# A two-block sequence model on one core: the products with 64 rows and 128 columns of weights in the two chunked recurrences, each made as two products of 64x64

## The chip, the cores and the metric

The kernel runs on one core of one Trainium2 chip, in float32 throughout. The metric is the device time of one execution in microseconds (us), the median of several. Below, PE is TensorE's matmul queue, PEld its weight loads, DVE is VectorE, ACT ScalarE, POOL GpSimd, SP the engine that issues the DMAs.

## The reference

Two blocks stand one behind the other, on 1024 tokens of width 1024. The first has two layers; each layer projects the normed input and runs three branches: a gated delta rule (GDN, 6 heads of 64), a latent attention (MLA) and an RWKV-7 recurrence (4 heads of 64). The second block is one with a gated convolution and a gated linear recurrence. The change touches the GDN and RWKV recurrences alone. The core of the GDN one, in chunks of c tokens, for both directions at once:

```
def step(s, inp):
    w_c, u0_c, p_c, qg_c, kd_c, ge_c = inp
    u = u0_c - jnp.einsum('nhcd,nhde->nhce', w_c, s)
    o = jnp.einsum('nhcd,nhde->nhce', qg_c, s) + jnp.einsum('nhij,nhje->nhie', p_c, u)
    s = ge_c[..., None, None] * s + jnp.einsum('nhcd,nhce->nhde', kd_c, u)
    return s, o
```

and the RWKV one, written token by token in the reference and made in chunks by the kernel:

```
sa = jnp.einsum('nhij,nhj->nhi', s, -kk_t)
s = s * w_t[:, :, None, :] + sa[..., None] * b_t[:, :, None, :] + v_t[..., None] * k_t[:, :, None, :]
y = jnp.einsum('nhij,nhj->nhi', s, r_t)
```

## The kernel before

The kernel works in stages with a barrier between them; in each layer of the first block the opening projections are followed by the stage `rw_chunk` (lines 722 to 1411, at 176 to 425 us of the span in layer 0), the GDN front, and the stage `gdn_chunk` (lines 1613 to 2237, at 573 to 890 us). Every engine runs its own written-out list of functions, and they meet by semaphore counts; the order of TensorE's list is the order of its work.

Both chunk stages cut the 1024 tokens into 8 chunks of 128 and take 8 steps s = 0 to 7; the forward direction takes chunk s and the backward one chunk 7 - s in the same step. A unit is a direction e and a pair of heads m: the two heads h = 0 and 1 of a pair lie in partitions 0 to 63 (LOW) and 64 to 127 (HIGH). RWKV has 4 units (8 products of one kind a step), GDN has 6 (12 products). A step consists of:

- `keys_on_state`: keys (weights, 64 rows of head width, 128 columns of tokens) times the state (64x64), added in the banks RB and RB + 1 to what `values_in` put there. In GDN `values_in` is the turning of the values, against a negative identity, of the same shape; in RWKV it is a product with 128 rows.
- `right_side` on ScalarE and VectorE copies the result out (R), `first_half` multiplies one half of the chunk by its inverse (64x64 products), the result is copied (W), `across` takes it to the other half (64x64), that is copied (R2), `second_half` multiplies again (64x64), and that is copied (W).
- `to_state` (128 rows, 64 columns) makes the new state, which VectorE copies or adds (Zc in RWKV, S in GDN); the next step's `keys_on_state` waits for it.
- `out_known` (RWKV) and `out_of_state` (GDN): queries (64 rows, 128 columns) times the old state, into the pair of banks of the step's output; `out_of_chunk` adds the part of the chunk itself (128x128 weights).

Steps 0 to 3 also hold the preparation of steps 4 to 7: `pairs` and `keys`, whose results VectorE masks and ScalarE takes apart (`take_out`, the rows of G, AT5, AT6). After steps 0 to 3 come `fill`, projections that cover VectorE's inverses of the next four chunks, and `join`, 32x32 products on four row groups in turn. Steps 4 to 7 have nothing of this kind in them. Pairs of banks are used in turn, by the list TURNS; `claim` waits until the last user's result has been copied out.

In the two heads h the output goes to bank b + h, so the two row halves write different banks.

Of the kernel before, what the change touches and what calls it, by code (L numbers as in the profile page):

```python
# [33 lines left out]
GH, GD = 6, 64  # L34
# [5 lines left out]
RH, RD = 4, 64  # L40
# [96 lines left out]
def build(nc, io, values):  # L137
    with ExitStack() as ctx:
# [23 lines left out]
        def sbuf(stack, name, shape, dt=F32):  # L162
            n = named.get(name, 0)
            named[name] = n + 1
            return stack.enter_context(nc.sbuf_tensor(f"{name}_again{n}" if n else name, shape, dt))
# [30 lines left out]
        ps = ctx.enter_context(nc.psum_tensor("ps", [P, 8, 512], F32))  # L196

        def cst(name, k=None):
            a, n = C_AT[name]
            return consts[:, a:a + n] if k is None else consts[:, a + k * P:a + (k + 1) * P]  # L200
# [21 lines left out]
        for L in range(DEPTH):  # L222
# [5 lines left out]
            with ExitStack() as st:  # L228
# [493 lines left out]
                with ExitStack() as st2:  # L722
# [4 lines left out]
                    KR = sbuf(st2, "KR_w", [P, 5, 4, 2, P])  # L727
# [29 lines left out]
                    Zc = sbuf(st2, "Zc_w", [P, 2, 4, RD])  # L757
                    rwm = sbuf(st2, "rwm", [P, 8 * P])
                    RB, WB, SB = 4, 6, 7
                    MID = P // 2  # L760
                    RATE = float(np.exp(-0.5))
                    LOW, HIGH = slice(0, 64), slice(64, 128)

                    def masked(s):
                        if s % 5 in (1, 2):
                            return mt_own[:, s % 5 - 1]
                        n = {0: 0, 3: 1, 4: 2}[s % 5] * 3072
                        return hflat[:, n:n + 3072].rearrange("p (u k n) -> p u k n", u=8, k=3)

                    def chunk(s, e):  # L770
                        return NT - 1 - s if e else s

                    def tok(s, e):
                        return slice(chunk(s, e) * P, chunk(s, e) * P + P)
# [29 lines left out]
                    def v_of(s, e, u):  # L804
                        return vt_all[:, chunk(s, e), RD * u:RD * u + RD]
# [16 lines left out]
                    with nc.Block() as block:  # L822
                        @block.tensor
                        def _(pe):
                            def claim(name):
                                old = used_before(name)
                                if old is not None and old[0] == "p" and old[1] != "c":
                                    pe.wait_ge(*VEC["MT" + old[1:]])
                                elif old is not None and old[0:2] == "kt":
                                    pe.wait_ge(*ACT[old])  # L830
                                elif old is not None and old[0:4] in ("fill", "late"):
                                    pe.wait_ge(*ACT[old])
                                elif old is not None and old[0:2] == "pc":
                                    pe.wait_ge(*(VEC if old[-1] == "1" else ACT)[old])
                                elif old is not None:
                                    pe.wait_ge(*ACT[old])
                                    pe.wait_ge(*VEC[old])
                                return pair_of_banks(name)
# [59 lines left out]
                            def keys_on_state(s):  # L898
                                pe.wait_ge(*VEC[f"Zc{s}"])
                                for em in range(4):  # L900
                                    for h in range(2):
                                        c0 = slice(64 * h, 64 * h + 64)
                                        q = pe.matmul(ps[:, RB + h, RD * em:RD * em + RD], lhsT=KR[c0, s % 5, em, 0, :], rhs=Zc[c0, s % 2, em, :], start=False,
                                                      stop=False, skip_group_check=True)
                                q.then_inc(*PE(f"R{s}"))

                            def first_half(s):
# [55 lines left out]
                            def out_known(s):  # L963
                                b = claim(f"o{s}")
                                for em in range(4):
                                    for h in range(2):
                                        c0 = slice(64 * h, 64 * h + 64)
                                        pe.matmul(ps[:, b + h, RD * em:RD * em + RD], lhsT=KR[c0, s % 5, em, 1, :], rhs=Zc[c0, s % 2, em, :], start=(em == 0),
                                                  stop=False, skip_group_check=True)
                                for em in range(4):  # L970
                                    for h in range(2):
                                        pe.matmul(ps[:, b + h, RD * em:RD * em + RD], lhsT=masked(s)[:, 2 * em + h, 2, :], rhs=v_of(s, em // 2, 2 * (em % 2) + h),
                                                  start=False, stop=False, skip_group_check=True)
# [38 lines left out]
                            for s in range(4):  # L1012
                                keys_on_state(s)
                                to_state_known(s)
                                pairs(s + 4, 0)
                                first_half(s)
                                pairs(s + 4, 1)
                                across(s)
                                pairs(s + 4, 2)
                                second_half(s)  # L1020
                                if s < 3:
                                    values_in(s + 1)
                                out_known(s)
                                to_state(s)
                                out_of_chunk(s)
                                pairs(s + 4, 3)
                                keys(s + 4)
# [389 lines left out]
            with ExitStack() as st:  # L1417
                gq = sbuf(st, "gq", [P, 9, SEQ])
# [8 lines left out]
                S = sbuf(st, "S_g", [P, 2, 6, GD])  # L1427
# [185 lines left out]
                with ExitStack() as st2:  # L1613
# [11 lines left out]
                    KQ = wflat.rearrange("p (a b m n) -> p a b m n", a=2, b=2, m=6)  # L1625
# [6 lines left out]
                    RB, WB, SB = 4, 6, 7  # L1632
# [22 lines left out]
                    LOW, HIGH = slice(0, 64), slice(64, 128)  # L1655
# [18 lines left out]
                    with nc.Block() as block:  # L1674
                        @block.tensor
                        def _(pe):
# [69 lines left out]
                            def values_in(s):  # L1746
                                for em in range(6):
                                    e, m = em // 3, em % 3
                                    for h in range(2):
                                        c0 = slice(64 * h, 64 * h + 64)  # L1750
                                        pe.matmul(ps[:, RB + h, GD * em:GD * em + GD], lhsT=gq[c0, 6 + m, tok(s, e)], rhs=cst("nident")[c0, c0], start=(em == 0),
                                                  stop=False, skip_group_check=True)

                            def keys_on_state(s):
                                pe.wait_ge(*VEC[f"KQ{s}"])
                                if s:
                                    pe.wait_ge(*VEC[f"S{s - 1}"])
                                for em in range(6):
                                    e, m = em // 3, em % 3
                                    for h in range(2):  # L1760
                                        c0 = slice(64 * h, 64 * h + 64)
                                        q = pe.matmul(ps[:, RB + h, GD * em:GD * em + GD], lhsT=KQ[c0, s % 2, e, 3 + m, :], rhs=S[c0, s % 2, em, :], start=False,
                                                      stop=False, skip_group_check=True)
                                q.then_inc(*PE(f"R{s}"))

                            def first_half(s):
# [48 lines left out]
                            def out_of_state(s):  # L1815
                                b = claim(f"o{s}")
                                for em in range(6):
                                    e, m = em // 3, em % 3
                                    for h in range(2):
                                        c0 = slice(64 * h, 64 * h + 64)  # L1820
                                        pe.matmul(ps[:, b + h, GD * em:GD * em + GD], lhsT=KQ[c0, s % 2, e, m, :], rhs=S[c0, s % 2, em, :], start=(em == 0),
                                                  stop=False, skip_group_check=True)

                            def out_of_chunk(s):
                                b = pair_of_banks(f"o{s}")
# [31 lines left out]
                            for s in range(4):  # L1857
# [4 lines left out]
                                if s < 3:  # L1862
                                    diff(s + 1, 1)
                            decays(0)
                            values_in(0)
                            for n in range(NT - 1):
                                fill(n)
# [2213 lines left out]
```

## Time and profile before

| | |
|---|---|
| time, median of 3 runs | 3975.13 us (3971.03 to 3977.76) |
| the profiled execution: its own time | 3983.26 us |
| its span | 3981.3 us |
| TensorE busy | 3652.6 us (92%), 24920 matmul records |
| TensorE weight loads | 2272.2 us (57%) |
| VectorE / ScalarE / GpSimd busy | 2247.3 (56%) / 1249.7 (31%) / 283.1 us (7%) |
| mean granted TensorE clock | 0.954 |

### The profile page before, as it was taken

The page shows a single profiled execution, that of the slowest core. Times are in us where ns is not written, and L with a number is a line of the kernel's source. Part 1 is how long each engine was busy: PE and PEld are TensorE (multiplying, and loading weights), DVE is VectorE, ACT ScalarE, POOL GpSimd, SP SyncE. Part 2 cuts the span into 40 slices and gives each one's busy share as a digit, 9 for nine tenths or more (in the row PEclk, how much of TensorE's full clock was granted, in tenths as well). Part 3 has the DMA queues.
Part 4 walks back from the last instruction along what each step waited for, and adds up shares of the span by engine and source line. Part 5 has one row for each costly group of instructions (what it writes and reads, how often), then busy time and mean ns, then how long its engine had stood idle before and what let it go on. Part 6 is the DMA issues. An engine that isn't in the chain of part 4 may idle for free. (4 is left out here: it accounts for less than half of the span.)

```text
span 3981.3 us, 60111 instructions
## 1 busy us (share of the span) xinstructions
PE 3652.6 (92%) x24920; PEld 2272.2 (57%) x24920; DVE 2247.3 (56%) x3955; ACT 1249.7 (31%) x2191; POOL 283.1 (7%) x233
## 2 busy tenths in 40 slices
PE   7889988988989979897997998899999997999999
PEld 4467535775654457744766664466666665444443
DVE  3475467835663456456764565356666667533453
ACT  3253354314531234245433453212222222231001
POOL 0010000000000011010000000022222222000000
PEclk9899999979999989998988999999999999999999
DMA  4223212102032333311212004211111110322331
GB/s 154 97 86 104 76 37 79 59 24 90 13 110 98 118 92 92 121 32 41 70 57 108 9 11 147 80 35 43 43 43 43 43 33 22 121 61 75 98 106 52
DMA packets 301822, 281.14 MB, mean 71 GB/s; under 512 B 18016, under 2 KB 274144, under 8 KB 301552
## 3 DMA queue, kind: packets, MB, share of 16 engines
q1 hardware_dynamic: 301552, 277.30, 21.6%
q8 instruction: 199, 3.26, 0.3%
q14 instruction: 71, 0.58, 0.0%
HBM read 203.93 MB, written 73.33 MB: 70 GB/s over the span
## 5 line engine op out<-in xcount | busy, mean ns | idle before, releaser
L3386 DVE SCALAR_TENSOR_TENSOR cv<-glu,params,cv 128x1024 f32<-128x1024 f32 x240 | 361.0, 1504 | 6.4
L1471 PE MATMUL ps<-hT,w_cols 128*128 128x512 f32 x576 | 254.9, 602 | 13.6 <-PEq L158 13.6
L399 PE MATMUL ps<-hT,w_cols 128*128 128x512 f32 x448 | 204.5, 617 | 3.3 <-PEq L158 3.3
L1471 PEld LDWEIGHTS ps<-hT,w_cols 128*128 128x128 f32 x576 | 110.9, 193 | 152.7 <-issue 150.8
L3682 PE MATMUL ps<-hT,wr 128*128 128x512 f32 x360 | 161.7, 592 | 0.0
L399 PEld LDWEIGHTS ps<-hT,w_cols 128*128 128x128 f32 x448 | 88.3, 199 | 116.4 <-issue 116.4
L3362 POOL TENSOR_TENSOR Sp<-Sp,Rp 128x520 f32<-128x520 f32 (+1 forms) x56 | 88.5, 1580 | 565.4 <-DVE W L3403 565.4
L3145 PE MATMUL ps<-hT,w_f 128*128 128x347 f32 x384 | 117.2, 465 | 6.8 <-DMA w_f<-in_w_in 6.8
L3160 PE MATMUL ps<-w_i,hT 128*128 128x128 f32 x1024 | 120.7, 277 | 0.0
L3682 PEld LDWEIGHTS ps<-hT,wr 128*128 128x128 f32 x360 | 68.4, 190 | 86.1 <-issue 86.1
L3160 PEld LDWEIGHTS ps<-w_i,hT 128*128 128x128 f32 x1024 | 116.1, 192 | 2.2 <-issue 1.6
L3145 PE MATMUL ps<-hT,w_glu_a 128*128 128x347 f32 x384 | 114.2, 456 | 0.4 <-ACT sgb L3326 0.4
L3152 PE MATMUL ps<-hT,w_g 128*128 128x512 f32 x256 | 114.1, 599 | 0.0
L2999 PE MATMUL ps<-w_out,mT 128*128 128x512 f32 x256 | 114.0, 604 | 0.0
L3145 PE MATMUL ps<-hT,w_glu_b 128*128 128x347 f32 x384 | 113.4, 454 | 0.0
L2999 PE MATMUL ps<-w_out_again,mT_again 128*128 128x512 f32 x256 | 113.2, 601 | 0.0
L3152 PE MATMUL ps<-hT,w_q 128*128 128x512 f32 x256 | 111.2, 592 | 0.0
L3682 PE MATMUL ps<-combos_even,sums_of_w 128*128 128x512 f32 x240 | 107.9, 592 | 0.0
L3145 PEld LDWEIGHTS ps<-hT,w_f 128*128 128x128 f32 x384 | 73.4, 193 | 46.8 <-DMA w_f<-in_w_in 7.2
L2506 PE MATMUL ps<-kT_again,qT_again 96*128 96x512 f32 x192 | 94.2, 614 | 2.1 <-PEq L158 2.1
L3365 POOL TENSOR_TENSOR Rp<-Rp 128x520 f32<-128x520 f32 (+1 forms) x56 | 95.3, 1702 | 4.4
L2506 PE MATMUL ps<-kT,qT 96*128 96x512 f32 x192 | 92.5, 605 | 2.1 <-PEq L158 2.1
(929 smaller groups left out, 7377.4 us busy)
## 6 DMA issues: line engine op xcount, KB each, us to landing
w_cols<-in_w_in SPq DMA_DIRECT2D x32, 512.0 KB, 3.9
wr<-in_w_in SPq DMA_DIRECT2D x24, 512.0 KB, 5.1
hT_hbm<-hT SPq DMA_DIRECT2D x2, 4096.0 KB, 14.1
hT<-hT_hbm SPq DMA_DIRECT2D x2, 4096.0 KB, 14.2
fh<-hT_hbm SPq DMA_DIRECT2D x16, 512.0 KB, 4.7
fh_again<-hT_hbm SPq DMA_DIRECT2D x16, 512.0 KB, 4.6
x<-in_x SPq DMA_DIRECT2D x8, 512.0 KB, 8.2
ahead<-kb_hbm SPq DMA_DIRECT2D x16, 256.0 KB, 3.3
```

The lines of the kernel that those rows point to most:

```text
L399: q = pe.matmul(ps[:, proj_bank(n, b), :], lhsT=wc[:, n % 3, k, :], rhs=hT[:, k, P + b * 512:P + (b + 1) * 512], start=(k == 0), stop=(k = ...
L1471: q = pe.matmul(ps[:, proj_bank(n, b), :], lhsT=wc[:, n % 3, k, :], rhs=hT[:, k, P + b * 512:P + (b + 1) * 512], start=(k == 0), stop=(k = ...
L2506: q = pe.matmul(ps[:, SCORES + 2 * (j % 2) + b, :], lhsT=qT[:, h, t * P:(t + 1) * P], rhs=kT[:, h, b * 512:(b + 1) * 512], start=True, sto ...
L2999: q = pe.matmul(ps[:, sum_bank(t, b), :], lhsT=mT[:, t % 2, k, :], rhs=wo[:, k, 512 * b:512 * (b + 1)], start=(k == 0), stop=(k == KD - 1))
L3145: q = pe.matmul(ps[:, BANK_X + b, 0:LONG], lhsT=wt[n][:, k, :], rhs=hT[:, k, T0 + b * LONG:T0 + (b + 1) * LONG], start=(k == 0), stop=(k = ...
L3152: q = pe.matmul(ps[:, bank + b, :], lhsT=wt[n][:, k, :], rhs=hT[:, k, P + b * 512:P + (b + 1) * 512], start=(k == 0), stop=(k == KD - 1))
L3160: q = pe.matmul(ps[:, BANK_X + b, (t % 3) * P:(t % 3 + 1) * P], lhsT=hT[:, k, t * P:(t + 1) * P], rhs=wt["i"][:, k, :], start=(k == 0), st ...
L3362: pool.tensor_tensor(S4[:, :, 0, :], S4[:, :, 0, :], R4[:, :, 1, (1 << k) - 1:1 << k].broadcast_to([P, n, 1 << k]), ALU.mult).then_inc(*PO ...
L3365: pool.tensor_tensor(R4[:, :, 1, :], R4[:, :, 1, :], R4[:, :, 0, (1 << k) - 1:1 << k].broadcast_to([P, n, 1 << k]), ALU.mult).then_inc(*PO ...
L3386: vec.scalar_tensor_tensor(out=cv[:, h % 2, :], in0=src, scalar=w, in1=cv[:, h % 2, :], op0=ALU.mult, op1=ALU.add).then_inc(*VEC(f"tap{h}_ ...
L3682: q = pe.matmul(ps[:, to, :], lhsT=a[:, k, :], rhs=b[:, k, :], start=(start and k == 0), stop=(k == 3), skip_group_check=True)
```

## The change

Each product with 64 rows and 128 columns of weights in five functions becomes two products of 64 rows and 64 columns: the first takes weight columns 0 to 63 and writes partitions 0 to 63 of the output, the second takes columns 64 to 127 and writes partitions 64 to 127. The moving operand, the banks, the waits and the semaphore counts stay as they are; the increment that closes `keys_on_state` sits on the last product of the last pair. The two products follow each other directly, ahead of the other row half. Products touched: 8 x 8 x 2 layers in each of RWKV's two functions, 12 x 8 x 2 in each of GDN's three, 832 in all, which become 1664. `pairs`, of the same weight shape, is not touched.

```
 # RWKV, keys_on_state
-q = pe.matmul(ps[:, RB + h, RD * em:RD * em + RD], lhsT=KR[c0, s % 5, em, 0, :], rhs=Zc[c0, s % 2, em, :], start=False,
-              stop=False, skip_group_check=True)
+for t in (LOW, HIGH):
+    q = pe.matmul(ps[t, RB + h, RD * em:RD * em + RD], lhsT=KR[c0, s % 5, em, 0, t], rhs=Zc[c0, s % 2, em, :],
+                  start=False, stop=False, skip_group_check=True)
 # RWKV, out_known
-pe.matmul(ps[:, b + h, RD * em:RD * em + RD], lhsT=KR[c0, s % 5, em, 1, :], rhs=Zc[c0, s % 2, em, :], start=(em == 0), ...
+for t in (LOW, HIGH):
+    pe.matmul(ps[t, b + h, RD * em:RD * em + RD], lhsT=KR[c0, s % 5, em, 1, t], rhs=Zc[c0, s % 2, em, :], ...
 # GDN, values_in
-pe.matmul(ps[:, RB + h, GD * em:GD * em + GD], lhsT=gq[c0, 6 + m, tok(s, e)], rhs=cst("nident")[c0, c0], start=(em == 0), ...
+for t in (0, 64):
+    here = slice(tok(s, e).start + t, tok(s, e).start + t + 64)
+    pe.matmul(ps[t:t + 64, RB + h, GD * em:GD * em + GD], lhsT=gq[c0, 6 + m, here], rhs=cst("nident")[c0, c0], ...
 # GDN, keys_on_state
-q = pe.matmul(ps[:, RB + h, GD * em:GD * em + GD], lhsT=KQ[c0, s % 2, e, 3 + m, :], rhs=S[c0, s % 2, em, :], start=False, ...
+for t in (LOW, HIGH):
+    q = pe.matmul(ps[t, RB + h, GD * em:GD * em + GD], lhsT=KQ[c0, s % 2, e, 3 + m, t], rhs=S[c0, s % 2, em, :], ...
 # GDN, out_of_state
-pe.matmul(ps[:, b + h, GD * em:GD * em + GD], lhsT=KQ[c0, s % 2, e, m, :], rhs=S[c0, s % 2, em, :], start=(em == 0), ...
+for t in (LOW, HIGH):
+    pe.matmul(ps[t, b + h, GD * em:GD * em + GD], lhsT=KQ[c0, s % 2, e, m, t], rhs=S[c0, s % 2, em, :], ...
```

## Rows read from the trace of the kernel before

**Rows 1.** The page, busy us of the engines (share of span), x instructions.
```profile
PE 3652.6 (92%) x24920; PEld 2272.2 (57%) x24920; DVE 2247.3 (56%) x3955; ACT 1249.7 (31%) x2191; POOL 283.1 (7%) x233
```

**Rows 2.** TensorE's timeline, RWKV step 0: start us, us, engine, line, records [idle before].
```profile
267.07 1.11 PE L903 MATMUL ps<-Zc_w,KR_w 64*128 64x64 f32 x16
268.11 0.70 PE L946 MATMUL ps<-Zc_w,consts 128*128 128x256 f32 x2
268.74 0.69 PE L950 MATMUL ps<-vt_all,KBt_w 128*64 128x64 f32 x16
269.36 1.14 PE L848 MATMUL ps<-KR_w,rw 64*128 64x256 f32 x8
270.42 0.27 PE L919 MATMUL ps<-R_w,Y_w 64*64 64x64 f32 x1
...
271.03 1.14 PE L848 MATMUL ps<-KR_w,rw 64*128 64x256 f32 x8
```

**Rows 3.** TensorE's timeline, RWKV's join, four row groups in turn.
```profile
259.37 2.00 PE L990 MATMUL ps<-w_cols 32*32 32x32 f32 x128
261.30 1.99 PE L878 MATMUL ps<-hT,yo_w 128*128 128x256 f32 x8
```

**Rows 4.** ScalarE's and TensorE's timelines, RWKV step 1, before `first_half`.
```profile
288.37 0.38 ACT L1115 ACTIVATE R_w<-ps 64x256 f32<-64x256 f32 x1
...
289.00 0.24 PE L919 MATMUL ps<-R_w,Y_w 64*64 64x64 f32 x1 [1.34 <-DVE hT L1224]
```

**Rows 5.** TensorE's timeline, RWKV step 4: `out_known`, and the step's one wait.
```profile
378.42 1.11 PE L968 MATMUL ps<-Zc_w,KR_w 64*128 64x64 f32 x16
...
382.68 0.24 PE L940 MATMUL ps<-R_w,Y_w 64*64 64x64 f32 x1 [0.61 <-DVE R_w L1237]
```

**Rows 6.** TensorE's timeline, GDN step 0.
```profile
674.95 0.27 PE L1777 MATMUL ps<-R_g,Y_g 64*64 64x64 f32 x1
...
675.80 0.70 PE L1716 MATMUL ps<-hT,consts 128*128 128x512 f32 x1
...
680.72 1.55 PE L1751 MATMUL ps<-consts,gq 64*128 64x64 f32 x24
682.11 0.67 PE L1726 MATMUL ps<-gq 64*128 64x128 f32 x8
683.63 0.92 PE L1811 MATMUL ps<-W_g,kd 128*64 128x64 f32 x24 [0.85 <-DVE PT L2052]
```

**Rows 7.** Timelines of three engines: before the first join; GDN steps 1 and 2.
```profile
655.38 2.91 PE L1841 MATMUL ps<-G_g,AT_g 32*32 32x32 f32 x192 [3.28 <-DVE G_g L2130]
...
704.49 0.54 DVE L2086 COPY W_g<-ps 64x384 f32<-64x384 f32 x1
...
712.13 0.49 ACT L1955 ACTIVATE o_g<-ps 128x384 f32<-128x384 f32 x1
713.14 2.16 ACT L1923 ACTIVATE G_g<-AT 32x192 f32<-32x192 f32 x4 [0.52 <-DVE AT L2046]
...
717.25 0.24 PE L1777 MATMUL ps<-R_g,Y_g 64*64 64x64 f32 x1 [0.65 <-ACT R_g L1937]
```

**Rows 8.** Timelines of TensorE and VectorE, GDN step 5, at the full clock.
```profile
841.63 0.24 PE L1787 MATMUL ps<-W_g,AT 64*64 64x64 f32 x1 [1.10 <-DVE W_g L2078]
842.48 1.55 PE L1821 MATMUL ps<-S_g,w_cols 64*128 64x64 f32 x24
842.58 0.55 DVE L2082 TENSOR_SCALAR R_g<-ps 64x384 f32<-64x384 f32 x1 [0.38 <-PE ps L1789]
843.96 0.27 PE L1798 MATMUL ps<-R_g,Y_g 64*64 64x64 f32 x1
```

**Rows 9.** TensorE's timeline, GDN step 4, at the lower clock.
```profile
816.64 2.82 PE L1821 MATMUL ps<-S_g,w_cols 64*128 64x64 f32 x24
```

**Rows 10.** Windows: stretch, length, busy (x) PE PEld DVE ACT POOL, granted clock, DMA.
```profile
807.00:830.40 23.40, 21.29 (x247) 19.66 (x246) 9.83 (x16) 6.46 (x10) 0.00 (x0) 0.70 0.03 10
2109.90:2126.90 17.00, 14.89 (x247) 13.57 (x246) 8.56 (x13) 3.22 (x6) 0.00 (x0) 1.00 0.07 25
```

More of the change, by code:

```diff
@@ L967, in out_known @@
                                         c0 = slice(64 * h, 64 * h + 64)
-                                        pe.matmul(ps[:, b + h, RD * em:RD * em + RD], lhsT=KR[c0, s % 5, em, 1, :], rhs=Zc[c0, s % 2, em, :], start=(em == 0),
-                                                  stop=False, skip_group_check=True)
+                                        for t in (LOW, HIGH):
+                                            pe.matmul(ps[t, b + h, RD * em:RD * em + RD], lhsT=KR[c0, s % 5, em, 1, t], rhs=Zc[c0, s % 2, em, :],
+                                                      start=(em == 0), stop=False, skip_group_check=True)
                                 for em in range(4):
@@ L1750, in values_in @@
                                         c0 = slice(64 * h, 64 * h + 64)
-                                        pe.matmul(ps[:, RB + h, GD * em:GD * em + GD], lhsT=gq[c0, 6 + m, tok(s, e)], rhs=cst("nident")[c0, c0], start=(em == 0),
-                                                  stop=False, skip_group_check=True)
+                                        for t in (0, 64):
+                                            here = slice(tok(s, e).start + t, tok(s, e).start + t + 64)
+                                            pe.matmul(ps[t:t + 64, RB + h, GD * em:GD * em + GD], lhsT=gq[c0, 6 + m, here], rhs=cst("nident")[c0, c0],
+                                                      start=(em == 0), stop=False, skip_group_check=True)
                             def keys_on_state(s):
@@ L1761, in keys_on_state @@
                                         c0 = slice(64 * h, 64 * h + 64)
-                                        q = pe.matmul(ps[:, RB + h, GD * em:GD * em + GD], lhsT=KQ[c0, s % 2, e, 3 + m, :], rhs=S[c0, s % 2, em, :], start=False,
-                                                      stop=False, skip_group_check=True)
+                                        for t in (LOW, HIGH):
+                                            q = pe.matmul(ps[t, RB + h, GD * em:GD * em + GD], lhsT=KQ[c0, s % 2, e, 3 + m, t], rhs=S[c0, s % 2, em, :],
+                                                          start=False, stop=False, skip_group_check=True)
                                 q.then_inc(*PE(f"R{s}"))
@@ L1820, in out_of_state @@
                                         c0 = slice(64 * h, 64 * h + 64)
-                                        pe.matmul(ps[:, b + h, GD * em:GD * em + GD], lhsT=KQ[c0, s % 2, e, m, :], rhs=S[c0, s % 2, em, :], start=(em == 0),
-                                                  stop=False, skip_group_check=True)
+                                        for t in (LOW, HIGH):
+                                            pe.matmul(ps[t, b + h, GD * em:GD * em + GD], lhsT=KQ[c0, s % 2, e, m, t], rhs=S[c0, s % 2, em, :],
+                                                      start=(em == 0), stop=False, skip_group_check=True)
                             def out_of_chunk(s):
```

## The prediction

> **What bounds the kernel now.** I read the page first for the share of each engine, then TensorE's timeline through the two recurrences, then the timelines of ScalarE and VectorE where TensorE stood still, and last the windows table for the granted clock. The page has TensorE busy for 92% of the span [rows 1]: time saved on it is time saved, unless something else was waited for at that place. The change touches five product groups of the two recurrences: `keys_on_state` and `out_known` of the first (RWKV), `values_in`, `keys_on_state` and `out_of_state` of the second (GDN). Each has 64 rows and 128 columns of weights and moves 64 columns, and each product stands as two records (8 products are x16) [rows 2]. RWKV groups have 8 products, GDN groups 12; a recurrence has 8 steps a layer, and there are two layers.
>
> **Price of a group.** Measured from a group's first start to the next group's first start. 64x128: 8 products take 268.11 - 267.07 = 1.04 us [rows 2]; 12 products 843.96 - 842.48 = 1.48 us [rows 8]; so 111 ns a product and 0.15 us fixed. 64x64, as the kernel already has it, with two quarters of the array in turn: 8 products 271.03 - 270.42 = 0.61 us [rows 2]; 12 products 675.80 - 674.95 = 0.85 us [rows 6]; 60 ns a product and 0.13 us fixed. So a quarter needs 120 ns for a product (two records), and a 64x128 product keeps its half busy for 222 ns, which fits weights loaded in proportion to their columns.
>
> The new groups have 16 and 24 products of 64x64, spread over all four quarters (low and high output for each row half). No row of before has four quarters of 64x64 in turn. The bounds: if all four run side by side, a product costs 120/4 = 30 ns, and the groups take 16 x 0.030 + 0.13 = 0.61 and 24 x 0.030 + 0.13 = 0.85 us, which with the later start of the third and fourth quarter I round to 0.62 and 0.86: 0.42 and 0.62 us saved a group. If only two run side by side, it is 60 ns: 1.09 and 1.57 us, 0.05 and 0.09 lost. If one runs at a time, 120 ns: 2.05 and 3.01 us, 1.01 and 1.53 lost. I take four side by side. Nearest rows: 64 products of 32x32 on four row groups in turn take 261.30 - 259.37 = 1.93 us, 30 ns each [rows 3], so TensorE can start records at the rate needed; products of 128x64 whose outputs alternate between the column halves while they share all rows take 269.36 - 268.74 = 0.62 us for 8 [rows 2], as quick as the 64x64 ones on separate rows. Column halves overlap, row halves overlap; the new form wants both at once.
>
> The Trainium skill, in "TensorE: Matmul & The Clock Gate" (Part 3, what overlaps and what doesn't), says that a weight load overlaps running matmuls only when the row group differs. Under it the two halves of one old product, which share rows, would not overlap, and the sum would be that of two side by side, near nothing. The 128x64 rows above, which share every row and overlap all the same, speak against it.
>
> **Neighbours.** A switch of form costs something: the same 12 products take 682.11 - 680.72 = 1.39 us when a 64x128 group follows [rows 6] and 1.48 when a 64x64 group does [rows 8], so 0.09 us. After the change `out_known` in steps 4 to 7 follows `first_half` (64x64) in its own form: 0.09 gained each. In GDN such gains (after `second_half`, around `out_of_state`) and losses (before `pairs`) fall mostly where TensorE waits; I put them at nothing, 0.2 us a step at most. "TensorEngine Tiling (Array Packing)" of the Trainium skill (Key Properties) says that a change of tiling mode drains TensorE; these two rows agree in sign, at 0.09 us.
>
> **What of the savings lies on the path.** By step:
> - RWKV, steps 0 to 3 (dense). `out_known` stands in a run of products without a wait: 0.42 each. `keys_on_state` saves in step 0. In steps 1 to 3 TensorE stands 1.34 us before `first_half`; the wait really ends with ScalarE's R copy, begun at 288.37, behind ScalarE's takeouts and the copy of the turned keys [rows 4]. That chain starts at the last `pairs` of the step before, ahead of `keys_on_state`: its 0.42 becomes longer waiting, three times a layer.
> - RWKV, steps 4 to 7. The only wait is 0.61 us before `second_half` [rows 5], for an answer to `across`; nothing changed lies in between. Both groups save in full.
> - Sum a layer: 5 x 0.42 + 8 x 0.42 + 4 x 0.09 = 5.8 us.
> - GDN, first `values_in`: the next inverse product waits 3.28 us for VectorE [rows 7], so nothing.
> - GDN, step 0: `keys_on_state` 0.62 in full, since everything after hangs on it. `values_in` is followed, one group later, by a wait of 0.85 us [rows 6]: nothing. `out_of_state`: nothing, ScalarE's takeouts run back to back from VectorE's earlier work until R.
> - GDN, steps 1 to 3: `to_state` waits for VectorE's W copy at 704.49 [rows 7], the end of a run of VectorE work without a gap, so `values_in` gives nothing. `first_half` waits 0.65 us for ScalarE's R [rows 7], so `keys_on_state` gives nothing. But that R comes right after a takeout begun at 713.14, which waited 0.52 us for VectorE's mask of the pairs that follow `out_of_state`; the 0.62 of `out_of_state` moves them all, until ScalarE's `out` copy (712.13 + 0.49) holds it: 713.14 - 712.62 = 0.52. The last of the three is passed on through VectorE's inverses.
> - GDN, steps 4 to 7: `keys_on_state` starts VectorE's chain that ends in the 1.10 us wait before `across` [rows 8]: 0.62. Between `across` and `second_half` stands `out_of_state` alone; shortened, it no longer covers the R copies (VectorE's from 842.58, 0.55 us [rows 8], then until TensorE starts the 0.25 that lie between the end of ScalarE's R, 288.75, and 289.00 [rows 4]): `second_half` at 843.38 instead of 843.96, 0.57. `values_in` likewise covers the W copies before `to_state`; I take 0.59 (not in step 7).
> - Sum a layer: 0.62 + 3 x 0.52 + 4 x (0.62 + 0.57) + 3 x 0.59 = 8.7 us.
>
> Both layers: 2 x (5.8 + 8.7) = 29 us. **Lower clock.** Steps of the GDN tail run partly at 1.2 GHz: a step with mean clock 0.70 took 23.4 us, one at 1.00 17.0 [rows 10]. There a changed group takes 2.82 us instead of 1.55 [rows 8 and 9], so halving its pace saves about 0.6 us more, three groups a step, about 3 such steps in both layers: 6 us. Against it, 1.2 us more of waiting comes into each of GDN steps 1 to 3 on top of the 0.65; the tail stands 2.1 us of 17 (17.00 - 14.89 [rows 10]), and its clock fell behind such waits. 14 us at the low level cost 6.4 (23.4 - 17.0): I allow for 11 us more of it, 5 us. The 1,664 further records (832 further products) on each of TensorE's two queues need no DMA worth naming.
>
> Total: 29 + 6 - 5 = 30 us. The profiled execution took 3983.26 us, so its like would take 3953; it stands 8 us above the median of the runs, 3975.13, and I forecast 3945 on that scale. Counted without any lost cover, 32 groups x 0.42 + 48 x 0.62 + 6 and the neighbours would be 50 to 54 us, 3925 to 3930: the low end.
>
> **Rivals.**
> - *Two side by side.* Quarters that share rows take turns. For it: no row has the 2x2 pattern, and one moving input must feed two column halves at different moments. Against: [rows 2]. The groups on the path (13 a layer in RWKV, 15 in GDN) lose 2 x (13 x 0.05 + 15 x 0.09) = 4 us, less the neighbours' 0.7 to 4: 3975 to 3979. Chance 0.13.
> - *The clock takes most of it.* The four quarters work, but the GDN steps 1 to 3 and parts of RWKV's tail drop to 1.2 GHz in stretches. Half of GDN steps 1 to 3 low (62 us in both layers) at 6.4/14 = 0.45 us for each costs, less what waits absorb, about 20: 3965. Chance 0.11.
> - *The clock, slower than before.* If all of both GDN front halves (2 x 82 us) stay low at the price 6.4/20.5 = 0.31 a us (waits absorb some), 51 us are lost against 35 gained: 3990. It decides from about 115 us of further low clock. For it: the tail already does this on the same share of waiting. Against: RWKV's tail does not. Chance 0.05.
> - *One at a time.* Each quarter's product waits for the one before it: on the same groups 2 x (13 x 1.01 + 15 x 1.53) = 72 us, so 4047. The overlaps in [rows 2, 3] speak against it. Chance 0.03.
>
> **How the numbers follow.** Forecast (3930 to 3960) 0.68. What can be told from no change here is about 0.2%, 8 us: 3967 to 3983. Faster: 0.68, plus 0.6 of the clock case, plus a little of two side by side (neighbours gained): 0.77. Same: 0.15. Slower: 0.08. Range 3930 to 3971, cutting into both first rivals.
>
> **What would show it.** The timeline after: 8 old products as 32 records in about 0.62 us, 12 as 48 in 0.86; 64x64 records of the two row halves and two column halves starting within some 30 ns of each other. RWKV tail steps shorter by 0.9 us; waits before `first_half` in RWKV steps 1 to 3 up from 1.34 to about 1.75, before GDN's `to_state` up by about 0.6. Wrong if the groups take 1.0 us or more, if the granted clock of the GDN front half falls below 1.00, or if steps shorten where I have them held.

## The result and the profile after

The changed kernel takes 3922.98 us (median of 4 runs, 3921.01 to 3925.38) against 3976.45 us for the kernel before (4 runs, 3971.03 to 3991.58): ratio 0.986, 95% interval 0.9832 to 0.9887, some 53 us gained where 30 were forecast. The profiled executions have spans of 3920.4 and 3981.3 us, 60.9 apart. Two of all executions below ran in a slower state of the chip, one of split_128 (5272.32 us) and the profiled one of stretch_after (4034.54 us, whose granted clock is 0.95 where the others have 1.00): they count in those two medians (without them 3881.24 and 3933.37), but in no ratio.

Part 1 of the page after, beside [rows 1]: TensorE has 832 x 2 = 1664 records more and 69 us less to do; the busy time of the other engines is the same to 0.2 us.

```profile
PE 3583.4 (91%) x26584; PEld 2207.4 (56%) x26584; DVE 2247.3 (57%) x3955; ACT 1249.5 (32%) x2191; POOL 283.3 (7%) x233
```

TensorE's timeline in RWKV step 0, against [rows 2] (start us, us, engine, line, operation, records, [idle before and its releaser]). The 8 old products are now 16, which stand as 32 records of 64x64, and take 267.41 - 266.78 = 0.63 us, where they took 1.04:

```profile
266.78 0.69 PE L904 MATMUL ps<-Zc_w,KR_w 64*64 64x64 f32 x32
267.41 0.70 PE L947 MATMUL ps<-Zc_w,consts 128*128 128x256 f32 x2
268.04 0.69 PE L951 MATMUL ps<-vt_all,KBt_w 128*64 128x64 f32 x16
```

The same in RWKV step 1 and step 4, against [rows 4] and [rows 5]: the wait before `first_half` has grown from 1.34 to 1.90 us, the one before `second_half` is 0.61 as before.

```profile
288.03 0.24 PE L920 MATMUL ps<-R_w,Y_w 64*64 64x64 f32 x1 [1.90 <-ACT R_w L1117]
...
380.84 0.24 PE L941 MATMUL ps<-R_w,Y_w 64*64 64x64 f32 x1 [0.61 <-DVE R_w L1239]
```

TensorE's timeline in GDN step 0, against [rows 6]: `values_in` (L1755) takes 674.43 - 673.53 = 0.90 us where it took 1.39, and the wait before `to_state` (L1816) is 1.53 us where it was 0.85. The wait grew by more than `values_in` saved, so nothing of that came through. The last row is `out_of_state` (L1827).

```profile
673.53 0.27 PE L1755 MATMUL ps<-consts,gq 64*64 64x64 f32 x2
...
674.43 0.71 PE L1728 MATMUL ps<-gq 64*128 64x128 f32 x8
676.68 0.92 PE L1816 MATMUL ps<-W_g,kd 128*64 128x64 f32 x24 [1.53 <-DVE PT L2058]
678.85 0.93 PE L1827 MATMUL ps<-S_g,w_cols 64*64 64x64 f32 x48 [0.16 <-DVE PT L2058]
```

TensorE's timeline in GDN step 6, whole step at the full clock, against [rows 8]: `keys_on_state` (L1767) takes 831.99 - 831.13 = 0.86 us; the waits before the second `pairs` (0.91) and before `across` (1.10) are untouched; `out_of_state` (L1827) and `values_in` (L1755) are the short groups.

```profile
831.13 0.93 PE L1767 MATMUL ps<-S_g,w_cols 64*64 64x64 f32 x48
831.99 1.53 PE L1744 MATMUL ps<-consts,gb 128*64 128x128 f32 x24
...
837.34 0.72 PE L1728 MATMUL ps<-gq 64*128 64x128 f32 x8 [0.91 <-DVE kd L2067]
839.15 0.24 PE L1792 MATMUL ps<-W_g,AT 64*64 64x64 f32 x1 [1.10 <-DVE W_g L2084]
839.87 0.90 PE L1827 MATMUL ps<-S_g,w_cols 64*64 64x64 f32 x44
841.44 0.27 PE L1755 MATMUL ps<-consts,gq 64*64 64x64 f32 x2
841.52 0.90 PE L1755 MATMUL ps<-consts,gq 64*64 64x64 f32 x46
842.48 0.92 PE L1816 MATMUL ps<-W_g,kd 128*64 128x64 f32 x24
843.33 2.89 PE L1837 MATMUL ps<-W_g,PT 128*128 128x64 f32 x24
```

Windows over GDN steps 4, 5, 6 of layer 0 and 4, 5 of layer 1 (stretch, length, busy (x) of PE, PEld, DVE, ACT, POOL, granted clock, DMA share, GB/s), against [rows 10]: a step at the full clock has gone from 17.0 to 15.0 us, and the steps whose mean clock was 0.70 are gone.

```profile
798.90:815.00 16.10, 13.90 (x319) 12.73 (x318) 9.89 (x16) 6.56 (x10) 0.00 (x0) 0.89 0.05 16
815.00:831.10 16.10, 13.99 (x319) 12.89 (x318) 8.56 (x13) 3.22 (x6) 0.00 (x0) 0.89 0.08 26
831.10:846.10 15.00, 12.79 (x319) 11.57 (x318) 8.56 (x13) 3.22 (x6) 0.00 (x0) 1.00 0.09 29
2019.40:2034.40 15.00, 12.79 (x319) 11.57 (x318) 9.88 (x16) 6.54 (x10) 0.00 (x0) 1.00 0.05 15
2034.40:2050.60 16.20, 14.01 (x324) 12.82 (x322) 8.56 (x13) 3.22 (x6) 0.00 (x0) 0.89 0.08 27
```

Where the 60.9 us of the two spans lie, by the starts of `keys_on_state` (steps 0 to 6 of each recurrence; step 7 stands with the stage behind it):

| stretch | layer 0 | layer 1 |
|---|---|---|
| RWKV steps 0 to 6 | -3.5 | -5.0 |
| RWKV step 7 up to GDN step 0 | -2.6 | -1.8 |
| GDN steps 0 to 3 and `fill`, `join` | -1.7 | -2.7 |
| GDN steps 4 to 6 | -17.9 | -12.8 |
| GDN step 7 and all up to the next RWKV step 0, or the end | -11.9 | -0.7 |

The remaining 0.3 us lie ahead of the first RWKV step.

The six GDN steps 4 to 6 give 30.7. At the full clock a step shortens by 16.98 - 15.03 = 1.95 us, 11.7 for six. The other 19.0 is the clock. Before, the six took 125.2 us where six at the full clock take 6 x 16.98 = 101.9: 23.3 us lost in 52.3 us at 1.2 GHz. After, 94.5 against 6 x 15.03 = 90.2: 4.3 us lost in 13.6. The low stretches begin around `across`: in all kernels here from 1.1 us ahead of its start to 2.1 us behind it, 7.6 to 12.1 us into a step. In the kernel before the three of these six steps last 20.5, 17.1 and 20.5 us and end in the next step, behind its `keys_on_state`; now each lasts 3.4. Of the 11.9 us behind GDN step 7 in layer 0, 3 to 11 are missing in every experiment below but stretch_after, also in three that gained nothing (thin_behind 4.7, dense_behind 6.1, no_out 7.3): the profiled execution before was long there, and its time lay 8 us above the median. So that row is mostly not the change's, and the 60.9 us overstate it; the medians say 53.

### The profile page after: what moved, and what is told of

It is laid out like the page before. It is cut to its first block and busy times, and to the rows that moved or that the text cites. A ratio compares the mean times of both kernels' runs of the same rounds, so it can differ in the third digit from the quotient of the medians.

```text
span 3920.4 us, 63439 instructions
## 1 busy us (share of the span) xinstructions
PE 3583.4 (91%) x26584; PEld 2207.4 (56%) x26584; DVE 2247.3 (57%) x3955; ACT 1249.5 (32%) x2191; POOL 283.3 (7%) x233
```

## The experiments

The question is what holds the clock in GDN steps 4 to 7. Theories:

- A, form: the new groups in these steps shorten the low stretches by what they are.
- B, place: the steps come earlier in the execution, and the low stretches fall elsewhere.
- C, length: the steps are shorter, whatever shortens them.
- D, form made precise: four-quarter work (64x64 products on all four quarters of the array) right behind the wait before `across` brings the clock back.
- E: the 64x128 group of `out_of_state`, which runs as the clock falls, keeps it low. F: more work between the waits keeps it low. (Both came up later.)

Times are medians; a ratio is to the kernel before on the same chip, with its 95% interval. "Low" is the time at 1.2 GHz in GDN steps 4, 5, 6 of layer 0 / of layer 1; in the kernel before 14.0, 6.4, 11.4 / 14.5, 6.0, 0. It comes from one profiled execution of each kernel, and the executions of one kernel differ (those of dense_behind took 3958.51 to 3997.01 us), so single stretches prove little; the medians stand beside them.

**rwkv_only, gdn_only: one recurrence each.** The two RWKV edits alone, and the three GDN edits alone.

> Only the two RWKV functions are split; GDN as before. After against before, the GDN tail (steps 4 to 7) lost its stretches at 1.2 GHz and that is some 20 us more than the prediction had. Theory A (form): the four-quarter groups of the tail themselves bring the clock back; then here GDN's tail keeps its low stretches (step 4 about 23.4 us, step 5 about 19.6) and the time is that of the RWKV groups alone, 2 x 5.8 = 12 us less: about 3964. Theory B (place in time): the tail's low stretches depend on when the tail begins; here it begins some 6 us earlier in layer 0, so its steps change by several us without any change in GDN, and the time could be anything from 3945 to 3970.

> Only the three GDN functions are split. Theory A (form): all of the clock's share is here: 2 x 8.7 = 17 us of priced savings plus some 20 to 25 of higher clock, about 3935; GDN tail steps 15 to 16 us. Theory B (place in time): the tail begins at another time than in the full change (RWKV's 6 us are missing), so low stretches may be back: 3945 to 3960.

rwkv_only: 3961.79 us, 0.9982 (0.9961 to 1.0003). Its RWKV steps shorten as in the changed kernel (0.83, 0.42, 0.42, then 0.99 each); its GDN steps start 7 us earlier in layer 0 and keep their long stretches: low 14.6, 5.9, 0 / 14.5, 6.0, 0, in layer 1 with the step lengths of before within 0.01 us. gdn_only: 3928.73, 0.990 (0.9881 to 0.9919); low 0, 0, 3.4 / 0, 3.4, 3.4. The two gains, about 7 and 40 us by the ratios, make 47 of the whole 53, which the intervals allow. B explains at most step 6 of layer 0, whose low stretch moved out.

**tail_only: the three GDN edits in steps 4 to 7 alone.**

```
 # keys_on_state; out_of_state likewise, and values_in with s >= 5
+if s >= 4:
+    for t in (LOW, HIGH):
+        q = pe.matmul(ps[t, RB + h, ...], lhsT=KQ[c0, s % 2, e, 3 + m, t], rhs=S[c0, s % 2, em, :], ...)
+else:
     q = pe.matmul(ps[:, RB + h, ...], lhsT=KQ[c0, s % 2, e, 3 + m, :], rhs=S[c0, s % 2, em, :], ...)
```

> The three GDN functions are split in steps 4 to 7 alone (values_in of steps 5 to 7). Steps 0 to 3 and RWKV as before, so the tail begins at the same time as before. Theory A: about 7 us a layer of priced savings (step at the full clock 15.0 instead of 17.0 us) and nearly all of the clock's share, 24 us: about 3938. Theory B: the tail begins where it began before, so the clock falls as before: only the priced part, 3961.

3938.99, 0.9925 (0.9902 to 0.9948): low 0, 3.4, 3.4 / 0, 3.4, 3.4, the six steps 94.8 us long against 125.2. The clock's gain is made in these steps by these edits.

**warm_before, warm_after: idle products in the waits.** No product is split in the first; the second is the changed kernel. In steps 4 to 7:

```
 pairs(s, 0, 0)
 first_half(s)
+3 idle products, 128x128 weights, 128 columns moved
 pairs(s, 1, 0)
+4 of them
 across(s)
```

> The kernel before, with idle products put into the two long waits of each GDN tail step (three 128x128 products moving 128 columns before the second pairs, four before across, into a bank that to_state overwrites; their result is used by nobody). Nothing is split. If the clock falls because of the waits (0.9 and 1.1 us) and stays down because the 64-column groups behind them are thin work, filling the waits keeps it up: the tail steps go to 17.0 us, low stretches gone, 24 us less in all: about 3952. If what matters is the form of the split groups and not the waits, the low stretches stay and the time is 3976 or a little more.

> The changed kernel with the idle products of warm_before in the two long waits of each GDN tail step. Both theories: the remaining low stretches of the tail (3.4 us each, 4 of them) go, steps 15.0 us each, 4 x 1.1 = 4 us less: about 3919. A version that could beat both.

warm_before: 3950.14, 0.9945 (0.9926 to 0.9965); six steps of 16.98, never low. So the low clock alone costs the kernel before some 22 us. warm_after: 3914.97, 0.985 (0.9812 to 0.9889), never low in these steps. The changed kernel has 0.986, with an interval that overlaps: what it still loses there is small.

**tail_out, tail_keys: one function each, in steps 4 to 7.** Only `out_of_state`, or only `keys_on_state`, in the new form. At the full clock they shorten a step by 0.68 and 0.62 us.

> Only out_of_state is split, in GDN steps 4 to 7 alone; it is the group right behind the 1.1 us wait. Priced part: 8 x 0.6 = 5 us. Theory D (form, right behind the wait): most of the clock's share comes too, low stretches of 3.4 us instead of 14 to 20, about 3955. Theory C (length of the step): the step is shortened by 0.6 us of 17 only, the clock behaves nearly as before, 3965 to 3970.

> Only keys_on_state is split, in GDN steps 4 to 7 alone; it stands at the head of the step, 8 us before the wait at which the clock falls. Priced part: 8 x 0.62 = 5 us. Theory D: it is too far from the wait to stop the fall, and cuts a low stretch only where it reaches it (the start of the next step): 3960 to 3967. Theory C: like tail_out, 3965 to 3970. If it gives as much as tail_out or more, D's 'right behind the wait' is wrong.

tail_out: 3949.46, 0.9945 (0.9923 to 0.9967), low 3.4, 3.4, 3.4 / 0, 0, 3.4. tail_keys: 3978.57, 1.0005 (0.9986 to 1.0024), low 13.3, 17.5, 17.5 / 0, 15.6, 4.9. Nearly the same work saved, and only the group behind `across` ends the long stretches; against C. That tail_keys would gain nothing at all no theory had foreseen (3960 to 3970).

**stretch_after, stretch_on_path: the changed kernel made long again.** VectorE gets three idle memsets a step, first beside its waits, then behind the waits for `keys_on_state` and `second_half`, so that they lengthen the path:

```
+vec.wait_ge(*PE[f"R{s}"])          # stretch_on_path alone
+vec.memset(idle, 0.0)              # 680 columns
 right_side(s)
 ...
+vec.memset(idle, 0.0)
 first_half(s)
 ...
+vec.wait_ge(*PE[f"w2_{s}"])        # stretch_on_path alone
+vec.memset(idle, 0.0)
 second_half(s)
```

> The changed kernel with three idle VectorE memsets (680 columns each) put into every GDN tail step, before the R copy and before both W copies, so that the step takes about as long as before the change (17 us instead of 15.0) with the same TensorE work. Theory C (length): the clock stays up after the change because the same work is packed into 15 us; stretched, the long low stretches (14 us in step 4) come back and tail steps take 20 us or more: about 3923 + 8 x 2 + 20 = 3959. Theory D (form): it stays up because the four-quarter groups right behind the waits are dense enough to bring the clock back within the shortest low stretch seen (3.4 us); then falls may be more frequent, the waits being longer, but each stays short: steps 17 to 18.5 us, about 3940 to 3948.

> stretch_after made the GDN tail step only 0.8 us longer at the full clock, since two of its three memsets ran where VectorE idled. Here they stand behind the waits for TensorE, so all three lengthen the step: 15.0 + 1.8 = 16.8 us, nearly the 17.0 of before, with the same split groups. Theory C: the long low stretches return, steps 19 to 24 us, 3955 or more. Theory D: low stretches of 3.4 us, perhaps in every step, steps 16.9 to 18.0: 3937 to 3945.

stretch_after: 3934.23, 0.9891 (0.9846 to 0.9935), low 0, 3.4, 3.4 / 0.2, 3.4, 3.4, and the step without low time 15.85 us, at that execution's granted clock of 0.95. It came back by 0.8 of the 1.95 us alone, so this run says little of C. stretch_on_path: 3941.59, 0.993 (0.9908 to 0.9952), 16.36 a step, with 3.3 to 3.5 us a step idle on TensorE (2.1 in the kernel before at the full clock); low 6.8, 0, 0 / 3.4, 3.4, 3.4. The stretches stay short. tail_keys is its counterpart: its step at the full clock is 16.36 us too, and its six steps had 68.8 us of low time where these have 17.0. At the same length the form decides: C falls.

**dense_behind, thin_behind: more work behind the wait.** The kernel before, with an idle group between `across` and its old `out_of_state` in steps 4 to 7 (its result is overwritten): 24 products of 64x64 on four quarters, or 12 of 64x128.

```
 across(s)
+extra(s)
 out_of_state(s)
 second_half(s)
```

> The kernel before, nothing split, with 24 idle 64x64 products in four quarters put between across and out_of_state in each GDN tail step (the same work as out_of_state, into the same banks, overwritten by it). They cost some 0.8 us a step, 6 us in all. Theory D (dense work right behind the wait brings the clock back): low stretches of 3.4 us instead of 14 to 20, tail steps 17.8 to 18.8 us, about 3957: faster than before although it does more. Theory C (the step must be short): the step is longer than before, the long low stretches stay, 3978 or more.

> The twin of dense_behind: the same idle work at the same place, as 12 products of 64x128 in two row halves. 1.4 us a step, 11 us in all. Theory D: this form is thin (a half of the array loads weights for most of the time), so the long low stretches stay: 3983 or more. If any further work behind the wait would do, it behaves like dense_behind: 3962.

thin_behind: 3995.45, 1.0057 (1.0036 to 1.0078), low 16.9, 7.0, 15.3 / 0, 15.3, 21.4: as expected of more old work. dense_behind: 3981.79, 1.0016 (0.9996 to 1.0037), a miss: low 15.1, 5.3, 3.4 / 0, 15.0, 5.5. The dense group stands right behind the wait, and two of three stretches still lasted 20.5 us; 3957 was expected, and the profiled execution (3971.76) was even a quick one of its ten. As I had put it, D is too simple. Three more runs.

**no_out, old_then_dense, dense_twice: what in dense_behind kept the clock low.** no_out: the kernel before without `out_of_state` in steps 4 to 7. old_then_dense: dense_behind with the two groups in the other order. dense_twice: tail_out with the idle dense group.

```
 across(s)
-out_of_state(s)        # no_out: nothing
                        # old_then_dense: out_of_state as it was, then 24 products of 64x64
                        #   that write the same values again
                        # dense_twice: 24 idle ones of 64x64, then out_of_state in the new form
 second_half(s)
```

> Kernel before, in which out_of_state is left out in GDN steps 4 to 7 (the output lacks that part). Two theories of why the stretches at 1.2 GHz in these steps are 14 to 20 us long before and 3.4 us with out_of_state in the new form. D: a group of four quarters right behind the wait before across brings the clock back; here there is none, so the long stretches stay (10 or more us low in most steps), about 3970. E: 64x128 products of out_of_state, which run as the clock falls, hold it low; here they are gone, so stretches of 3.4 to 6.8 us at most and steps of 16.4 to 18 us, about 3950.

> dense_behind in the other order: the 64x128 out_of_state right behind across, and the idle 64x64 group behind it. E: as dense_behind, long stretches in at least three of the six steps, 3975 to 3990. D, read as any four-quarter group soon after the fall: stretches of 3.4 to 6.8 us, about 3957.

> tail_out (only out_of_state in the new form, in GDN steps 4 to 7) with a second, idle group of 24 products of 64x64 between across and out_of_state: the work behind the wait is as long as in dense_behind less 0.62 us a step, without its 64x128 group. D and E: stretches of 3.4 us at most, steps of 17.2 at the full clock and 18.4 with one stretch, 3949 + 8 x 0.86 = about 3956. F, that more work between the waits is what held the clock low in dense_behind: long stretches again, 3970 or more.

no_out: 3979.74, 1.0019 (1.0003 to 1.0035), low 12.3, 16.8, 16.8 / 11.9, 16.9, 17.0, more than in any other kernel, with less work: E falls as the whole cause. D had about 3970 for it. dense_twice: 3945.27, 0.9935 (0.9913 to 0.9957), low 3.4, 3.4, 0 / 0, 0, 0, with as many groups as dense_behind: F falls. old_then_dense: 3969.58, 0.9992 (0.9971 to 1.0013), low 6.8, 6.8, 6.8 / 0, 6.8, 6.8: the stretches are those of D, the time lies between D's 3957 and E's 3975.

The shortest low stretches last 3.4 us. The first 3.4 us of the others, set beside them as windows (same columns as above), tell more. The kernel before, where the old `out_of_state` fills most of it; the clock stayed low:

```profile
816.40:819.80 3.40, 3.40 (x39) 3.17 (x37) 0.55 (x1) 0.49 (x1) 0.00 (x0) 0.50 0.00 0
```

The changed kernel, with `across`, the new `out_of_state` and part of `second_half`; the clock rose behind it:

```profile
806.60:810.00 3.40, 3.02 (x85) 3.06 (x87) 1.47 (x3) 0.49 (x1) 0.00 (x0) 0.50 0.02 5
```

tail_out, the same, and the next 3.4 us, at the full clock:

```profile
819.60:823.00 3.40, 3.40 (x87) 3.28 (x82) 1.10 (x2) 1.22 (x3) 0.00 (x0) 0.52 0.02 5
823.00:826.40 3.40, 3.40 (x57) 3.26 (x56) 1.35 (x3) 3.15 (x4) 0.00 (x0) 0.98 0.00 0
```

no_out, low in both and on; the second is busy throughout with old `values_in` and `to_state`:

```profile
811.90:815.30 3.40, 2.67 (x46) 2.39 (x41) 1.09 (x3) 0.92 (x2) 0.00 (x0) 0.51 0.00 0
815.30:818.70 3.40, 3.40 (x44) 3.28 (x44) 0.12 (x1) 3.34 (x5) 0.00 (x0) 0.50 0.00 0
```

old_then_dense: low behind the first (the old group), up behind the second (mostly the dense group and `second_half`):

```profile
812.10:815.50 3.40, 3.40 (x47) 3.17 (x46) 0.55 (x1) 0.49 (x1) 0.00 (x0) 0.50 0.00 0
815.50:818.90 3.40, 3.40 (x78) 3.28 (x72) 0.55 (x1) 0.94 (x2) 0.00 (x0) 0.50 0.02 5
```

dense_behind, two different stretches: the first stayed low, the second rose. Both hold the dense group, but of the old `out_of_state` the first holds 2.02 us and the second 1.31:

```profile
811.70:815.10 3.40, 3.40 (x74) 3.28 (x67) 0.55 (x1) 0.48 (x1) 0.00 (x0) 0.50 0.00 0
...
856.10:859.50 3.40, 3.40 (x79) 3.28 (x76) 0.74 (x2) 0.48 (x1) 0.00 (x0) 0.50 0.02 5
```

The changed form doesn't always suffice. In stretch_on_path TensorE stands 1.81 us before `across`; one of its low stretches begins 1.1 us ahead of `across` and holds more of that wait than the others do. Its first 3.4 us, with the new `out_of_state` in them, stayed low, and the clock rose 3.4 us later:

```profile
804.40:807.80 3.40, 2.25 (x64) 2.28 (x67) 2.22 (x4) 0.48 (x1) 0.00 (x0) 0.51 0.03 5
```

The reader is to see two things. PE stands busy for 3.40 of 3.40 us in windows behind which the clock stayed down and for 3.02 in one behind which it rose, so the busy column doesn't tell these apart. What does is what ran: windows filled mostly with 64x64 work (the dense group or the new `out_of_state`, and `second_half`) were followed by the full clock, and windows with the old 64x128 group, or with a gap in its place, were not. dense_behind, where the dense group shares the time with the old one, went either way, and in stretch_on_path a window with 1.15 us idle stayed low with the new form in it. That is D with its condition corrected: not what stands first behind the wait, but what TensorE runs over the whole time. This reading was made after the runs and tested by none of its own. The other end fits no simple rule either: the stretches of 17.1 us and more, in all kernels here, ended in the next step, among its `keys_on_state` and the groups behind it (in GDN step 5 of the kernel before at 836.9 us, behind L1742). What exactly the chip counts stays open.

**split_all, split_128: the same split for the other wide products.** The changed kernel, with every product of 128 rows and 128 columns of weights that moves 64 columns (RWKV `values_in`, `out_of_chunk` and the second part of `out_known`, GDN `out_of_chunk`) made as two of 128x64; split_all has the idle products of warm_after too.

```
-q = pe.matmul(ps[:, b + h, ...], lhsT=PT[:, 6 * e + u, :], rhs=W[:, e, ...], ...)
+for t in (LOW, HIGH):
+    q = pe.matmul(ps[t, b + h, ...], lhsT=PT[:, 6 * e + u, t], rhs=W[:, e, ...], ...)
```

> warm_after with the products of 128x128 weights and 64 moving columns made as two of 128x64 as well (RWKV values_in, the second part of out_known, out_of_chunk; GDN out_of_chunk). Before they take 1.93 us for 8 and 2.82 for 12; as two column halves in turn, by the 128x64 rows (0.62 us for 8), 1.08 and 1.55. RWKV: 3 groups x 0.85 x 8 = 20 us a layer, nearly all on the path; GDN: 1.27 a step in the tail, less in steps 0 to 3 where ScalarE and VectorE bind, 6 to 8 us a layer. About 3915 - 54 = 3861; to 3885 if the copies of ScalarE and VectorE come to bind.

> split_all without its idle 128x128 products: the kernel after, with the products of 128 rows and 128 columns of weights that move 64 columns made as two of 128x64 as well. If the gain of split_all over after (46 us) is that second split: 3880 to 3890, the 8 us that warm_after gained over after missing. If much of it is the clock: above 3895.

split_all: 3877.21, 0.9764 (0.9748 to 0.978). split_128: 3882.01, 0.9771 (0.9746 to 0.9796): the second split gives 41 us on top of the change by the medians, 35 by the ratios; the idle products give nothing that can be told. Both beat the changed kernel, whose interval starts at 0.9832. TensorE's timeline of split_128 in GDN step 4: the 12 products of `out_of_chunk` take 796.52 - 794.99 = 1.53 us, where in the timeline of step 6 above they take 846.15 - 843.33 = 2.82 (846.15 is the start of the next `keys_on_state`, which follows at once).

```profile
794.27 0.92 PE L1819 MATMUL ps<-W_g,kd 128*64 128x64 f32 x24
794.99 1.60 PE L1841 MATMUL ps<-W_g,PT 128*64 128x64 f32 x48
796.52 0.50 PE L1770 MATMUL ps<-S_g,w_cols 64*64 64x64 f32 x17
```

Windows over its GDN steps 4 to 6, layer 0 and layer 1: 13.8 us a step, never low.

```profile
782.90:824.40 41.50, 34.46 (x1031) 30.80 (x1030) 27.02 (x42) 12.90 (x22) 0.00 (x0) 1.00 0.08 27
1981.10:2022.70 41.60, 34.49 (x1029) 30.79 (x1028) 27.01 (x42) 12.98 (x22) 0.00 (x0) 1.00 0.08 27
```

In the RWKV tail the second split brings a new cost. Steps 4, 5 and 6 of layer 0 take 8.4, 9.5 and 12.8 us, where the changed kernel has 11.25 each: in step 6 TensorE stops twice in the middle of a group, for 1.93 and 1.94 us, and the profile shows nothing that it waits for ("issue"). The changed kernel has no such stop there. What makes them no run here settles.

```profile
384.30 0.33 PE L905 MATMUL ps<-Zc_w,KR_w 64*64 64x64 f32 x2 [1.93 <-issue]
```

## Why the prediction was wrong

The direction and the mechanism of the groups were right; the time, 3922.98, fell below the range, which ended at 3930.

- *Price of a group.* Forecast 0.62 and 0.86 us, measured 0.625 and 0.858. All four quarters run side by side: inside a group a record starts about every 15 ns at the full clock. The rule of "TensorE: Matmul & The Clock Gate" in the Trainium skill (Part 3, what overlaps and what doesn't), that a weight load overlaps running matmuls only when the row group differs, I had read as making the two halves of an old product take turns, for 1.09 and 1.57 us; the measured times decide against that. Both rivals with fewer quarters are out.
- *RWKV.* Forecast 0.93 a step in the tail, measured 0.99. In steps 1 and 2 forecast 0.42 each with the wait before `first_half` at about 1.75; measured 0.27 to 0.42 and 1.90. Step 0: forecast 0.84, measured 0.83. rwkv_only gained about 7 us where the steps make 2 x 5.8; its interval (-1 to 15) holds both.
- *GDN steps 0 to 3.* Forecast 0.62 in step 0 and 0.52 in each of steps 1 to 3, 2.18 a layer; measured in layer 0 1.11, -0.02, 0.61 and 0.02 (1.7), in layer 1 -0.16, 1.29, 0.64 and 0.95 (2.7). The sums come near, the steps don't: step 0 of layer 0 gained 0.49 more than I had, and step 1 nothing; gdn_only has the same two (1.12 and -0.03). Step 0 of layer 1 had 3.4 us at the low clock in it. Which wait I misread there was not worked out. The wait before `to_state` in step 0 grew by 0.68, forecast about 0.6. Otherwise the granted clock stayed full in steps 0 to 2, and step 3, with `fill` and `join`, has 6.8 us low in both kernels. Neither clock rival came.
- *GDN steps 4 to 6, work.* Forecast 0.62 + 0.57 + 0.59 = 1.78 a step at the full clock, measured 1.95.
- *The failed step is the clock term.* The prediction had "14 us at the low level cost 6.4 (23.4 - 17.0): I allow for 11 us more of it, 5 us", and set 6 us of gain against that, from changed groups running in the same low stretches as before: 1 us of gain in sum. Measured in the six steps, the low time fell from 52.3 to 13.6 us, and that was worth 19.0. The price was right: 23.3 us for 52.3, 0.45 us each, as 6.4 for 14. The amount of low time had the wrong sign. I read the low stretches as the work of the waits ("its clock fell behind such waits"), and more waiting as more low time. The waits do stand at the fall, with 1.10 us before `across` in both kernels, and with both waits filled it never came (warm_before). But the length of the stretch hangs on what TensorE does behind it, and the change alters just that, in `out_of_state`. tail_out shows it alone: a group shorter by some 0.6 us, low time down from 52.3 to 13.6 us, and 0.9945 of the time.
- *What the trace before would have told.* [rows 9] is the place: the old `out_of_state` at 2.82 us in the first 3.4 us of the stretch. That its form set the length of the stretch could not be read there: no row had the new form in such a place. RWKV's tail, with an old 64x128 group too but one wait of 0.61 us a step [rows 5], never fell; I had counted it as evidence against a rival only.
- The sum with the clock as measured: 30 - 1 + 19 = 48, to which comes 1 us of more saved work in the six steps; the median gain is 53 (45 to 67 by the interval). The rest is within what these runs can tell.
- *The low end.* "50 to 54 us, 3925 to 3930" is a slip: from 3975.13 it gives 3921 to 3925, so the range ended above its own sum. The measured 3922.98 lies in the corrected figures by luck. That sum lets all 48 GDN groups save in full and gives the clock nothing, and of the 53 us some 19 are the clock's.

## What to carry to other kernels

Where 64 columns are moved per weight load, as here, a product with 128 columns of weights cost 1.7 to 1.8 times what its two halves of 64 columns cost (1.48 against 0.86 us for 12 of 64 rows, 2.82 against 1.53 for 12 of 128): cut such products into column halves, as split_128 does with both, and look for new stops of TensorE behind it. When a stage runs partly at the lower clock, look at where each low stretch starts and what TensorE runs in it, and price a change to that group by the whole stretch, not by the group. Idle products in the waits can keep the clock too (warm_before), but the new form of the same work brought nearly all of that without them.

## What the runs showed of the hardware

- Four 64x64 quarters at once: 16 float32 products (32 records) in 0.625 us, 24 (48 records) in 0.858.
- 128 rows and 128 columns of weights against 64 moved columns: 12 products 2.82 us; as 24 of 128x64, 1.53.
- The granted clock fell around the same place of a GDN step (from 1.1 us ahead of the start of `across` to 2.1 us behind it) in every kernel but warm_before, warm_after, split_all and split_128, where it stayed full. It came back after 3.4 us, after 6.8, or after 17 to 24, by what ran meanwhile. The form of one group of 12 products took the low time of six steps from 52.3 to 13.6 us (tail_out).
- Removing that group (no_out) made the kernel no faster: 1.48 us less work a step, and 39 us more low clock in six steps.
- Low time costs less than half of itself: 23.3 us for 52.3, 0.45 for each, in the six steps of the kernel before.
- With the second split (split_128), TensorE stopped twice for 1.9 us in one step of RWKV's tail, with nothing shown that it waited for.
